# A longer seven-product stretch in the second feed-forward block, and two moves in the token mixing

## The reference, cut to what matters

```
x += 0.5 * SwiGLU_1(RMSNorm(x))          # D_FF = 2816: gate and up 1024 -> 2816, down 2816 -> 1024
x += token_mixing(RMSNorm(x))            # 4 heads of a gated linear recurrence, and a short convolution
x += CrossAttn(RMSNorm(x), RMSNorm(mem)) # 4 heads, 256 memory tokens
x += 0.5 * SwiGLU_2(RMSNorm(x))
RMSNorm(x)
```

## Time and profile before

| | |
|---|---|
| median of 3 runs | 1118.38 us (1118.32 to 1120.45) |
| profiled execution, its own time | 1120.16 us |
| its span, first to last instruction | 1118.2 us |
| TensorE busy | 1106.8 us, 99% |
| VectorE, ScalarE, GpSimd busy | 626.9, 522.2, 437.1 us |

### The profile page before, as it was taken

How to read it: one execution, slowest core, us unless ns; L and a number is a source line. 1 busy time by engine, 2 the same in 40 slices (tenths; PEclk the granted TensorE clock), 3 DMA queues, 4 the chain that set the end, 5 groups by cost and what they waited for, 6 DMA issues and landing times.

```text
span 1118.2 us, 17287 instructions
## 1 busy us (share of the span) xinstructions
PE 1106.8 (99%) x6358; PEld 971.0 (87%) x6358; DVE 626.9 (56%) x911; ACT 522.2 (47%) x725; POOL 437.1 (39%) x544
## 2 busy tenths in 40 slices
PE   9999999999999999999999999999999999999997
PEld 7889999988888888888888888888889999988886
DVE  6887777441222668888567123464787777440012
ACT  6545555542323555654466443354455555542221
POOL 0000000486665544434548883173000000485651
PEclk9999999999999999999999999999999999999999
DMA  7276775332323221222313442122187675332312
GB/s 240 76 210 188 194 197 169 114 112 96 113 94 111 77 76 57 76 76 76 113 57 133 163 157 76 39 81 102 45 226 188 178 197 169 114 113 96 112 57 76
DMA packets 48626, 135.33 MB, mean 121 GB/s; under 512 B 4672, under 2 KB 10944, under 8 KB 48448
## 3 DMA queue, kind: packets, MB, share of 16 engines
q1 hardware_dynamic: 43344, 118.38, 30.2%
q0 software_dynamic: 4032, 14.68, 7.7%
q10 hardware_dynamic: 1200, 1.57, 0.4%
HBM read 132.52 MB, written 2.10 MB: 120 GB/s over the span
## 4 chain that ended last, share of the span: by engine, by line
PE 53%; POOL 25%; issue 21%; DVE 0%; POOLq 0%; DMA 0%; ACT 0%; DVEq 0%; SPq 0%; ACTq 0%
POOL wl L438 25%; PE bank L1420 9%; PE bank L1422 9%; PE bank L1421 9%; PE bank L1522 4%; PE bank L1524 4%; PE bank L1523 4%; PE score L1523 3%; PE score L1522 3%; PE score L1524 3%; PE o_bank L1522 1%; PE o_bank L1524 1%; PE o_bank L1523 1%; PE bank L1479 1%; PE bank L1483 1%
## 5 line engine op out<-in xcount | busy, mean ns | idle before, releaser
L438 POOL TENSOR_TENSOR wl<-raw,wh 128x256 fp32r<-128x256 f32 x512 | 412.5, 839 | 326.0 <-ACT wh L472 281.8
L472 ACT ACTIVATE wh<-raw 128x1024 fp32r<-128x1024 f32 x124 | 130.1, 1054 | 162.2 <-PE bank L1422 158.1
L1420 PE MATMUL bank<-xh,wh 128*128 128x512 f32 x488 | 194.8, 399 | 0.0
L1422 PE MATMUL bank<-xh,wl 128*128 128x512 f32 x488 | 190.4, 390 | 0.0
L1421 PE MATMUL bank<-xl,wh 128*128 128x512 f32 x488 | 190.1, 390 | 0.0
L452 POOL DMA_DIRECT2D raw<-w_all x28 | 24.3, 869 | 330.1 <-DMA raw<-w_all 330.1
L1420 PE MATMUL bank<-zr,wh 128*128 128x512 f32 (+1 forms) x374 | 142.6, 381 | 0.0
L1422 PE MATMUL bank<-zr,wl 128*128 128x512 f32 (+1 forms) x374 | 141.7, 379 | 0.0
L1421 PE MATMUL bank<-zr,wh 128*128 128x512 f32 (+1 forms) x374 | 140.5, 376 | 0.0
L902 DVE SCALAR_TENSOR_TENSOR x<-bank,x 128x512 f32<-128x512 f32 (+1 forms) x31 | 21.3, 687 | 175.4 <-PE bank L1422 175.4
L1421 PEld LDWEIGHTS bank<-xl,wh 128*128 128x128 f32 x488 | 91.8, 188 | 19.9 <-issue 1.7
(11 more groups left out here) (304 smaller groups left out, 2493.8 us busy)
## 6 DMA issues: line engine op xcount, KB each, us to landing
raw<-w_all SPq DMA_DIRECT2D x200, 512.0 KB, 3.3
raw<-w_all POOLq DMA_DIRECT2D x28, 512.0 KB, 5.2
zf<-w_all SPq DMA_DIRECT2D x28, 256.0 KB, 4.5
x<-x_t SPq DMA_DIRECT2D x8, 256.0 KB, 6.2
out_t<-x SPq DMA_DIRECT2D x8, 256.0 KB, 2.4
raw<-w_all SPq DMA_DIRECT2D x6, 256.0 KB, 6.1
memf<-mem_t ACTq DMA_DIRECT2D x1, 1024.0 KB, 4.8
raw<-w_all ACTq DMA_DIRECT2D x2, 256.0 KB, 3.9
```

The source lines that it names most:

```text
L438: ins = nc.gpsimd.tensor_tensor(wl[:, slot, two], raw[:, slot, two], wh[:, slot, two].bitcast(f32), SUB)
L472: nc.scalar.activation(wh[:, slot, :], raw[:, slot, :], ACT.Copy).then_inc(hi_ready, 1)
L1420: nc.tensor.matmul(out_, a[0], b_[0], start=first, stop=False)
L1422: return nc.tensor.matmul(out_, a[1], b_[0], start=False, stop=last)
```

## The change

It has three parts.

1. The order of units in the mixing: head 3's q moves from slot 18 to slot 16, in front of C 1 and u 1, which move to slots 17 and 18.
2. VectorE's `differences(h, 6)` moves in step L2 behind `factors(h, 4)` and `factors(h, 5)`, and `factors(h, 6)` moves from L2 to step K, behind the copies of levels five and six.
3. PRE, ST and OLD become lists, one entry for each feed-forward block. The first block keeps 6, 14 and 4. The second has 4 plain column blocks (two of them with x that is not normalised), and 16 pairs. ScalarE and VectorE get an own order for the opening of this block, and the sum of squares goes behind column 0's first seven chunks.

```diff
 MIX_SLOTS = [("f", 0), ("q", 0), ("v", 0), ("v", 1), ("v", 2), ("v", 3),
              ("f", 1), ("q", 1), ("g", 0), ("C", 0), ("u", 0), ("f", 2),
-             ("B", 0), ("q", 2), ("f", 3), ("g", 1), ("C", 1), ("u", 1),
-             ("q", 3), ("g", 2), ("g", 3), ("B", 1), ("C", 2), ("u", 2), ("B", 2), ("C", 3), ("u", 3), ("B", 3)]
+             ("B", 0), ("q", 2), ("f", 3), ("g", 1), ("q", 3), ("C", 1),
+             ("u", 1), ("g", 2), ("g", 3), ("B", 1), ("C", 2), ("u", 2), ("B", 2), ("C", 3), ("u", 3), ("B", 3)]
...
-PRE = 6
-ST = 14
-OLD = 4
-P_UNIT = 2 * (PRE + ST)
+NF = 20
+PRE = [6, 4]
+ST = [NF - n for n in PRE]
+OLD = [n - 2 for n in PRE]
+P_UNIT = 2 * NF
...
ScalarE, opening of a feed-forward block:
-                if which == 1:
-                    ahead(u0)
                 inverse_root(norm, rstd[:, :], n_bank[:, :], D)
+                ahead(u0)
                 if which == 0:
...
+                else:
+                    silu(0)
+                    ahead(u0 + 1)
+                    ahead(u0 + 2)
+                    for i in range(4):
+                        x_split(i)
+                    silu(1)
+                    ahead(u0 + 3)
+                    for o in range(4):
+                        t_split(o)
+                    silu_new(2)
+                    ahead(u0 + 4)
+                    g2_split(u0 + 2 * pre + 1, 16 * (1 + ST[0] // 2 * which), u0 + 6)
+                    a22_split(0, 16 * (1 + ST[0] // 2 * which), u0 + 5)
+                    silu_new(3)
...
VectorE, opening of a feed-forward block:
+                else:
+                    x_norm(0)
+                    x_norm(1)
+                    gate(0)
+                    up(0)
+                    for k in range(2, 6):
+                        x_norm(k)
+                    dve.wait_ge(lo_ready, u0 + SLOTS)
+                    unit_low(u0 + 4)
+                    hid_old(0)
+                    x_norm(6)
+                    x_norm(7)
+                    unit_low(u0 + 5)
+                    for i in range(4):
+                        x_low(i)
+                    gate(1)
+                    up(1)
+                    unit_low(u0 + 6)
+                    hid_old(1)
+                    t_make(0)
+                    t_make(1)
+                    unit_low(u0 + 7)
+                    t_make(2)
+                    t_make(3)
+                    for o in range(4):
+                        t_low(o)
+                    hid_direct(2, tiles(zf, HID + 2))
+                unit_low(u0 + 2 * pre)
+                unit_low(u0 + 2 * pre + 1)
                 sums_make(0, n0, False)
                 a22_low(0, n0)
-                hid_direct(5, tiles(zf, HID + 5))
+                hid_direct(pre - 1, tiles(zf, HID + pre - 1))
...
VectorE, steps of the mixing:
                     if (h, a) != (0, 0):
                         differences(h, 2 * a)
                         differences(h, 2 * a + 1)
-                    if a == 2:
-                        differences(h, 6)
                     if a > 0:
                         take_scores(h, 2 * a - 2)
                         take_scores(h, 2 * a - 1)
                     factors(h, 2 * a)
                     factors(h, 2 * a + 1)
                     if a == 2:
-                        factors(h, 6)
+                        differences(h, 6)
                 if kind == "K":
...
                     take_scores(h, 4)
                     take_scores(h, 5)
+                    factors(h, 6)
                     dve.wait_ge(exp_ready, EXPS * h + DIFFS)
...
TensorE, opening of the second block:
-                    sum_squares(norm, qn + KC)
+                            elif c == 0:
+                                sum_squares(norm, qn + KC)
                     for c in range(2, 4):
                         group(u0 + c, g0 + c)
...
```

More of the change, by code:

```diff
@@ L402, in pairs @@
             def pairs(u0, which):
-                for j in range(ST):
-                    u, p = u0 + 2 * (PRE + j), j % 2
+                for j in range(ST[which]):
+                    u, p = u0 + 2 * (PRE[which] + j), j % 2
                     if j < 2:
@@ L526, in ffn @@
                 u0, g0, hb = (U_FFN1, G_UP1, 0) if which == 0 else (U_FFN2, G_UP2, FC)
-                n0 = ST * which
+                n0 = ST[0] * which
+                pre, st, old = PRE[which], ST[which], OLD[which]
                 def silu(j):
@@ L621, in ffn @@
[L621 to L634, removed]
@@ L635, in ffn @@
-                with act.Fori(0, (ST - 2) // 2) as i:
+                    silu(0)
[4 more added lines that the diff above has]
+                    ahead(u0 + 4)
+                    ahead(u0 + 5)
+                    silu(2)
+                    for i in range(4):
+                        x_split(i)
+                    silu(3)
+                    t_split(0)
+                    ahead(u0 + 6)
+                    ahead(u0 + 7)
@@ L1042, in ffn @@
                 norm_of(norm)
[L1043 to L1070, removed]
-                    t_make(o)
-                unit_low(u0 + 10)
-                t_low(0)
-                t_low(1)
-                hid_direct(4, tiles(zf, HID + 4))
@@ L1507, in ffn @@
                                 last.then_inc(unit_used, 1)
-                    sum_squares(norm, qn + KC)
+                            elif c == 0:
+                                sum_squares(norm, qn + KC)
                     for c in range(2, 4):
-                        group(u0 + c, g0 + c)
-                n0 = ST * which
-                for c in range(4, 2 * OLD):
-                    group(u0 + c, g0 + c, release=x_old if c == 2 * OLD - 1 else None)
-                for c in range(2 * OLD, 2 * PRE):
-                    group(u0 + c, g0 + c, ready=(xn_lo, KC * which) if c == 2 * OLD else None)
+                        group(u0 + c, g0 + c, release=x_old if c == 2 * old - 1 else None)
+                for c in range(4, 2 * old):
+                    group(u0 + c, g0 + c, release=x_old if c == 2 * old - 1 else None)
+                for c in range(2 * old, 2 * pre):
+                    group(u0 + c, g0 + c, ready=(xn_lo, KC * which) if c == 2 * old else None)
                 def seven(out_, a, at, b_, cols_, first):
```

145 lines of the change are left out of this document (92 added, 53 removed).

## The result

The changed kernel takes 1126.24 us (median, 1125.85 to 1127.98) against 1118.38 (1118.32 to 1120.45) of the kernel before: a ratio of 1.0065, 95% interval 1.0053 to 1.0077. It is slower by 7.9 us where 4.5 were forecast.

The account below looks back on a forecast made before the run. TensorE, busy 1106.8 of 1118.2 us, was taken to bound the kernel. Mixing waits less the second block's saving summed to +4.5 us, median 1122.9; own range 1120.0 to 1125.6, 8 in 10 range 1117.5 to 1126.5.

Parts of the forecast that it names:

- the clock: TensorE's clock in the mixing: the sum took it to stay full through the waits and added nothing for it.
- head 1: Mixing, head 1: most of the 0.79 us level five wait goes, 0.3 us comes back a step later; -0.4 us.
- head 2, level seven: Mixing, head 2's level seven product: TensorE waits for late root, copies, moved factors and the query's reading; +4.2 us.
- head 3, level one: Mixing, head 3's first factors no longer hang on a late query, so the 0.99 us wait goes; -1.0 us.
- head 3, level three: Mixing, head 3: the convolution's four operations now stand behind the first factors, so part of the gain returns; +0.5 us.
- head 3, level seven: Mixing, head 3: the late root, copies and moved factors repeat without the query; TensorE waits, +3.2 us.
- second block: Second feed-forward block: two hidden columns move from plain units to seven-product pairs, no stall; -2.0 us.
- rival (c): Second block: eight units too short for VectorE's list, a 1 to 3 us stall before the first pair, 1125; chance 0.08.
- the forecast's shortest case: Heads 2 and 3: level seven's exponential only 1.15 us later, with every form of VectorE's operations fast, instead of 1.7.
- Rival (a): Mixing: VectorE has the lead after all, old waits go and no new ones come; -3.8 us, 1114.6; chance 0.13.
- Rival (b): Mixing: only the query costs, delayed exponential hidden at head 3, half hidden at head 2; near 1118.1, no change; chance 0.12.
- rival (d): Mixing, head 2: the clock halves at the 4.2 us stand, adding 1.8 us to the sum, 1124.7; chance 0.10.

Follow-up runs that it names:

- kernel 7: Kernel before plus the second block's longer stretch and level seven moved at heads 0 and 1 only, old order of units: 1117.73 us, ratio 0.9980.
- kernel 1: Kernel before plus only the second block's longer stretch; order of units and level seven as before: 1117.52 us, ratio 0.9982.
- kernel 2: Changed kernel with head 3's query back in slot 18, level seven still moved: 1127.09 us, ratio to before 1.0058.
- kernel 5: Changed kernel, but at heads 2 and 3 ScalarE computes the previous head's root before level seven's exponential: 1117.26 us, ratio to before 0.9976.
- kernel 3: Changed kernel without the level seven move, query still in slot 16: 1117.90 us, ratio to before 0.9981.
- Kernel 4: Changed kernel plus filler matmuls of ones on TensorE before level seven's scores, 14 at head 2 and 11 at head 3: 1124.08 us, ratio to before 1.0037.
- 8: kernel 7 with head 3's query in slot 17, one slot earlier than before: 1116.08 us, ratio to before 0.9973.
- 10: kernel 9 with the four operations of u 1's convolution moved behind the steps of slot 19: 1116.83 us, ratio to before 0.9974.
- kernel 9: kernel 5 with head 3's query in slot 17 instead of 16: 1117.16 us, ratio to before 0.9974.
- 6: Changed kernel with level seven's subtractions back ahead of the copies, only its factors moved: 1122.47 us, ratio to before 1.0022.

## Why the prediction was right, and which term was too small

The direction, the places and the mechanism of the waits were right. The time, 1126.24, lies 0.3 us below the top of the range for 8 in 10, but above the sum's own range, which ended at 1125.6: what the sum added up does not reach it. The term that failed is the clock, which the sum put at nothing.

TensorE runs the same matmuls in the same order through the mixing of both kernels, so the loss can be read product by product, each start counted from the sum of squares ahead of the mixing:

| place | forecast, us | measured, us |
|---|---|---|
| head 1 | -0.4 | -0.4 |
| head 2, level seven | +4.2 | +3.8 |
| half clock behind it | none | +1.7 |
| head 3, level one | -1.0 | -1.2 |
| head 3, level three | +0.5 | +0.6 |
| head 3, level seven | +3.2 | +3.1 |
| half clock behind it | none | +1.7 |
| second block | -2.0 | -2.0 |
| sum | +4.5 | +7.35 |

- **Second block.** The sum of squares was put at 766.1; it stands at 773.73, and the kernel is 7.62 us late there (VectorE's last addition moved from 763.97 to 771.59), so at 766.1 on the old count. The x lows were to start at 781.3: 788.98 less 7.62 is 781.36. No wait before the first pair, so rival (c) is out.
- **Head 1.** Its level five starts 0.7 us sooner and its level seven 0.4, in after and in kernel 7 alone, whose whole stretch is 0.42 us shorter than kernel 1's.
- **Head 2.** VectorE's idle time for the root was put near 3.4: 3.36. But the exponential was to be 1.7 us late, and counted from the sum of squares the norm behind the root is 1.0 us later than in before: the moved subtractions took 0.41 us each, as in the forecast's shortest case (1.15). The wait is 3.72 us, because TensorE, ahead by head 1's gain, asked 0.5 us sooner. Without the query it is 2.73 (kernel 2), so the query's share is 1.0, not 1.3 to 1.4.
- **The root behind the exponential** makes the chain long, and not the amount of work: kernel 5 shows it. Rival (a) counted on VectorE having a lead; at head 2 the 0.46 us that it idled for the root already said no. Rival (b) would have needed small waits at level seven without the query; kernel 2 has 2.73 twice.
- **What the query buys.** Alone, it does at head 3 what the forecast said (kernel 3: -1.1 and +0.6). But in after the -1.0 is not its doing: kernel 2 loses the level one wait without it, because TensorE comes later there. So beside level seven's move the query only costs: 1.0 us at head 2's wait and 0.6 at level three. The sum for after is not touched by this, but the reason given for the -1.0 was wrong.
- **The clock.** Kernel 4, with the clock held, is at +4.2 us against before, near the forecast's +4.5. The other 3.2 us of the +7.35 are rival (d), which had a chance of 0.10 and was priced at +1.8 for head 2 alone. Its price was right and its count was wrong: it came at head 2 and at head 3, after 2.95 us, a wait that the forecast did have in its sum (3.2) but did not hold up against the clock. With (d) at both places the forecast would have read 8.1 us and a median of 1126.5; that this is so near 1126.24 is in part luck, since the waits were 0.6 us less than forecast.

The step behind it was the reading of the earlier trace rows, where the clock is full for 3 us while TensorE does nothing. TensorE's last matmul before that window ends at 1111.59,

```profile
1110.89 0.70 PE L1631 MATMUL o_bank<-sq,ones 128*128 128x256 f32 x2 [0.53 <-ACT sq L826]
```

and the clock falls between 1115 and 1118.2: late, and with TensorE idle throughout. At head 2 of after the clock is full, too, up to the end of the wait (485.25) and falls behind it, when TensorE works again. A clock that is full during a wait does not say that it will be full behind it.

## What to carry to other kernels

Before a piece of work is moved later on one engine, look up what stands behind it on the engine it feeds: here two subtractions of 0.4 us and two factors, moved later, made TensorE wait 3.7 and 3.0 us, because another head's root was queued behind their exponential, and putting that root first took the whole loss away (kernel 5). A forecast wait of the sizes seen here (2.2 us and more) needs a second term for the clock, here 1.7 us and once 3.4, which the waits don't show: compare the duration of the same matmul before and behind the wait. And where VectorE has no lead at several products in a row, moving one unit of its work can just move the wait (kernels 3, 8 and 10), while taking it from in front of the one product that waits can win (kernel 9 against 5).

## What the runs showed of the hardware

The granted clock of TensorE behind a wait in the mixing:

| idle time, us | kernel, place | clock after it |
|---|---|---|
| 0.99 | before, head 3 | full |
| 1.19 | 6, head 3 | full |
| 2.17 | 6, head 2 | 0.5 for 3.4 us |
| 2.73 | 2, head 2 | 0.5 for 3.4 us |
| 2.73 | 2, head 3 | 0.5 for 6.8 us |
| 2.95 | after, head 3 | 0.5 for 3.4 us |
| 3.72 | after, head 2 | 0.5 for 3.4 us |

The half clock costs half of its length, 1.7 or 3.4 us. Two equal waits of 2.73 us cost 1.7 and 3.4 us, in one execution; what tells them apart was not tried. One thing differs in the rows: at head 2 the first eight matmuls behind the wait still run at full clock (1.11 us), at head 3 they don't (1.97). No wait between 1.19 and 2.17 us was seen, and the table has one execution of each kernel: the times of kernels 2 and 6 suggest that the same waits do not always bring the same falls. With the filler matmuls in both waits, the clock stayed full (kernel 4).
